# Two distances from the weights, modulo 256 bytes, for the operands of the split fp32r matmuls

## The chip, the cores and the metric

The kernel runs on one core of a Trainium2 chip. The metric is the device time of one execution in microseconds, on the slowest core, which here is the only one. Three timed executions of the kernel before took 1705.59, 1720.77 and 1727.60 us; their median, 1720.77 us, is the time before. A fourth execution was profiled.

## What is computed

Two transformer blocks over one sequence of 256 tokens of width 1024, in float32. What matters for this change are the six feed-forward stages; between them stand three mixers (an mLSTM with a spatial gating unit, a pooling and SSD mixer, and a latent attention) and two final norms.

```python
def swiglu(x, w_in, w_out):
    gate, up = jnp.split(x @ w_in, 2, axis=-1)
    return (jax.nn.silu(gate) * up) @ w_out

x = x + 0.5 * swiglu(rmsnorm(x, ffn1_norm_g[l]), ffn1_w_in[l], ffn1_w_out[l])
```

`D_MODEL` is 1024 and `D_FF` is 2816, so one stage multiplies the 256 tokens by 1024 x 5632 and by 2816 x 1024 weights.

## The kernel before

**Stages.** `PHASES` lists eleven stages, numbered n = 0 to 10: feed-forward stages at n = 0, 2, 4, 6, 7 and 9, the mixers at 1, 5 and 8, the final norms at 3 and 10. Activations lie transposed: channels on the 128 partitions, tokens along the free dimension, so `x` is 128 x 8 x 256.

**Weights.** They come as one stream of blocks of 128 x 2048 float32 (1 MB each). A feed-forward stage has 33 blocks: 11 steps of one gate block, one up block and one out block. Each block is loaded into one of three slots of `raw`. ScalarE then rounds it to fp32r into `whi` (line 176), and VectorE writes the rest, `raw - whi`, into `wlo` (line 184).

**Split matmuls.** To keep float32 precision, each product is made of three fp32r matmuls, `PASSES`: high weights by high activations, high weights by low activations, low weights by high activations. In `pe_in` (line 252, gate and up) the moving operand is `xh`, `xl`, `xh` in turn; in `pe_out` (line 284) it is `hid_hi`, `hid_lo`, `hid_hi`. The stationary operand is a 128 x 128 piece of `whi` or `wlo`. Each matmul has its own weight load and streams 256 columns of 4 bytes. One block is 48 such matmuls, and a stage is 33 x 48 = 1584, the six stages 9504. The first gate block of a stage goes through line 244, in another order of the same three products.

**What sets the order.** It is written out by hand with semaphores, and in a feed-forward stage steps 1 to 10 are five turns of a hardware loop of two steps each (`pe.Fori(1, 5)` after a first turn). In a step TensorE runs gate, up and out blocks one behind the other without a pause if the blocks are split in time.

**Where the tiles lie.** SBUF addresses follow the order of the declarations. In bytes of one partition, `whi` and `wlo` start 24,576 apart (a multiple of 256), `xh` starts 88,512 bytes behind `whi` and `xl` 8,192 further; `hid_hi` starts 132,800 bytes behind `whi` and `hid_lo` 4,096 further. 88,512 and 132,800 are both 192 more than a multiple of 256. The pieces of a weight block start at multiples of 512 bytes and the rows of the activations at multiples of 1,024, so in every matmul of lines 244, 252 and 284 the moving operand lies 192 bytes, modulo 256, behind the stationary one. `hid_hi` and `hid_lo` are tiles of a region that the mixers use again for their own tiles; those lie at the same distance of 192. In `pe_tok` (line 267) the roles are exchanged, the weights stream and `xh`, `xl` are stationary, so there the moving operand is at distance 64.

Of the kernel before, what the change touches and what calls it, by code (L numbers as in the profile page):

```python
# [29 lines left out]
P = 128  # L30
T = 256
D = 1024
KD = D // P
# [23 lines left out]
MOD_GROUPS = {0: 5, 1: 5, 2: 5, 3: 3, 4: 0, 5: 0}  # L57


PARAMS = [("g_ffn1", 8), ("g_mix", 8), ("g_ffn2", 8), ("g_final", 8), ("conv_w1", 64), ("conv_b1", 16),  # L60
          ("b_i", 1), ("b_f", 1), ("head_g", 8), ("sgu_bs", 128), ("mod_b", 144), ("norm_g2", 48),
          ("pool_scale", 4), ("conv_w2", 48), ("conv_b2", 12), ("dt_bias", 1), ("a_log", 1), ("ssd_d", 8),
# [6 lines left out]
def offsets(table):  # L69
    at, o = {}, 0  # L70
    for name, width in table:
        at[name] = (o, o + width)
        o += width
    return at, o


def build_program(nc, a_x, a_pos, a_stream, a_mod, a_params, a_consts, a_sgu, a_out, phases=PHASES):
    F32, F32R, I32 = mybir.dt.float32, mybir.dt.float32r, mybir.dt.int32
    ALU, ACT, AX = mybir.AluOpType, mybir.ActivationFunctionType, mybir.AxisListType
    ds = bass.ds  # L80
    P_AT, P_N = offsets(PARAMS)
    C_AT, C_N = offsets(CONSTS)
    first_block, b0 = [], 0
    for _, _, nb in phases:
        first_block.append(b0)
        b0 += nb
# [3 lines left out]
    with ExitStack() as ctx:  # L90
        def sb(name, shape, dt=F32):
            return ctx.enter_context(nc.sbuf_tensor(name, shape, dt))
# [3 lines left out]
        def sem(name):  # L96
            if name not in sems:
                sems[name] = ctx.enter_context(nc.semaphore(name))
            return sems[name]
# [5 lines left out]
        mod_raw = sb("mod_raw", [P, 2, BLK])  # L105
        mod_acc = sb("mod_acc", [P, D])
        mod_tab = sb("mod_tab", [P, 144])
        mod_part = sb("mod_part", [P, 5, 32])
        fold = sb("fold", [P, 32])
        ident_b = sb("ident_b", [P, P], mybir.dt.bfloat16)  # L110
        mask_b = sb("mask_b", [P, P], mybir.dt.bfloat16)
# [6 lines left out]
        xm = sb("xm", [P, KD, T])  # L118
        gmod = sb("gmod", [P, KD])
        gres = sb("gres", [P, KD])  # L120
        xh = sb("xh", [P, KD, T], F32R)
        xl = sb("xl", [P, KD, T], F32R)
        std = sb("std", [P, T])
        rstd = sb("rstd", [P, T])
        params = sb("params", [P, P_N])
# [8 lines left out]
        def region(**tensors):  # L134
            with ExitStack() as here:
                return [here.enter_context(nc.sbuf_tensor(name, shape, dt)) for name, (shape, dt) in tensors.items()]

        gate, hid, hid_hi, hid_lo, mod_turned = region(gate=([P, 2, T], F32), hid=([P, 2, T], F32),
                                                       hid_hi=([P, 2, 2, T], F32R), hid_lo=([P, 2, 2, T], F32R),
                                                       mod_turned=([P, 32, 32], F32))  # L140


        bank = [ctx.enter_context(nc.psum_tensor(f"bank{i}", [P, 512], F32)) for i in range(8)]
# [10 lines left out]
        def cst(name):  # L154
            lo, hi = C_AT[name]
            return consts[:, lo:hi]
# [202 lines left out]
        def pe_norm(pe, n):  # L359
            if n > 0 and phases[n - 1][0] == "final":  # L360
                pe.wait_ge(sem("x_updated"), 4 * n)
            for b in range(4):
                if b == 0 and n > 0:
                    pe.wait_ge(sem("silu_done"), STEPS * sum(kind == "ffn" for kind, _, _ in phases[:n]))
                if b >= 2:
                    pe_keep_warm(pe, n, WARM[b - 2])
                pe.wait_ge(sem("x_paired"), 4 * n + b + 1)
                for tt in range(2):
                    mm = pe.matmul(STAT[:, T + tt:T + tt + 1], xm[:, 2 * b, tt * P:tt * P + P], ones[:, 0:1],  # L369
                                   start=(b == 0 and tt == 0), stop=(b == 3), skip_group_check=True)  # L370
            mm.then_inc(sem("x_summed"), 1)
            pe_keep_warm(pe, n, WARM[2])
            pe.wait_ge(sem("rstd_ready"), n + 1)
            for tt in range(2):
                mm = pe.matmul(STAT[:, tt * P:tt * P + P], rstd[:, tt:tt + 1].to_broadcast([P, P]), ident,
                               start=(tt == 0), stop=True, skip_group_check=True)
            mm.then_inc(sem("rstd_spread"), 1)
            if phases[n][0] != "final":
                pe_keep_warm(pe, n, WARM[3])
            elif n + 1 < len(phases):  # L380
                pe_keep_warm(pe, n, 60)
# [53 lines left out]
        for n, (kind, idx, _) in enumerate(phases):  # L435
            if kind != "final":
                split_index[n] = k_split
                k_split += 1
                if kind in ("mix2", "mix3"):
                    shift_index[n] = k_shift  # L440
                    k_shift += 1
# [184 lines left out]
        group0, g = {}, 0  # L626
# [1339 lines left out]
        @block.sync  # L1966
        def _(sp):
            for i in range(2):
                sp.dma_start(x[:, 4 * i:4 * i + 4, :], a_x[:, 4 * i:4 * i + 4, :]).then_inc(sem(f"x_loaded{i}"), 16)
            sp.dma_start(consts[:, :], a_consts).then_inc(sem("consts_loaded"), 16)  # L1970
            sp.dma_start(params[:, 0:4 * KD], a_params[:, 0:4 * KD]).then_inc(sem("consts_loaded"), 16)
            for n in range(min(SLOTS, N_BLOCKS)):
                sp.dma_start(raw[:, n, :], a_stream[n * P:n * P + P, :]).then_inc(sem(f"w_loaded{n}"), 16)
            sp.dma_start(params[:, 4 * KD:P_N], a_params[:, 4 * KD:P_N]).then_inc(sem("params_loaded"), 16)
            full = N_BLOCKS // SLOTS

            def load(s, turn):
                sp.wait_ge(sem("w_lo_ready"), s - SLOTS + 1 + SLOTS * turn)
                sp.dma_start(raw[:, s, :], a_stream[ds(s * P + SLOTS * P * turn, P), :])\
                  .then_inc(sem(f"w_loaded{s}"), 16)  # L1980

            if full > 1:
                with sp.Fori(1, full) as turn:
                    for s in range(SLOTS):
                        load(s, turn)
            for s in range(N_BLOCKS % SLOTS):
                load(s, full)
            sp.wait_ge(sem("x_updated"), 4 * (len(phases)))
            sp.dma_start(a_out, x[:, :, :]).then_inc(sem("stored"), 16)
            sp.wait_ge(sem("stored"), 16)  # L1990
# [32 lines left out]
        @block.tensor  # L2023
        def _(pe):
            pe.wait_ge(sem("zeros_ready"), 1)
            for _ in range(60):
                pe.matmul(GATE[:, 0:P], row_parts[:, 0:P], row_parts[:, 0:P], start=True, stop=True)
            pe.wait_ge(sem("consts_loaded"), 32)
            pe.wait_ge(sem("masks_ready"), 3)
            for n, (kind, f, _) in enumerate(phases):  # L2030
                if n == 1:
                    pe.wait_ge(sem("params_loaded"), 16)
                PE[kind](pe, n, f)

        @block.scalar
        def _(act):
            act.wait_ge(sem("eps_ready"), 2)
            for n, (kind, f, _) in enumerate(phases):
                ACTS[kind](act, n, f)

        @block.vector
        def _(dve):
            dve.memset(row_parts[:, :], 0.0).then_inc(sem("zeros_ready"), 1)
            dve.memset(cols[:, 64:65], RMS_EPS).then_inc(sem("eps_ready"), 1)
            dve.memset(cols[:, 65:66], LN_EPS).then_inc(sem("eps_ready"), 1)
            dve.wait_ge(sem("consts_loaded"), 32)
            dve.tensor_copy(ident_b[:, :], ident).then_inc(sem("masks_ready"), 1)
            dve.tensor_copy(mask_b[:, :], cst("maskT")).then_inc(sem("masks_ready"), 1)
            dve.tensor_copy(row_of3[:, :], cst("row_of3")[0:96, :]).then_inc(sem("masks_ready"), 1)
            dve.tensor_reduce(fold[:, :], ident.rearrange("p (q i) -> p i q", q=4), AX.X, ALU.add)\  # L2050
               .then_inc(sem("fold_ready"), 1)
            for n, (kind, f, _) in enumerate(phases):
                DVE[kind](dve, n, f)


# [59 lines left out]
def _params(v):  # L2115
# [11 lines left out]
    def conv(w):  # L2127
# [16 lines left out]
          "sgu_wT": v["sgu_w_s"][0].transpose(2, 0, 1).reshape(P, -1)}  # L2144
    return np.concatenate([at[name].reshape(P, width) for name, width in PARAMS], axis=1)

# [44 lines left out]
```

## Time and profile before

| | before |
|---|---|
| median of 3 executions | 1720.77 us (1705.59 to 1727.60) |
| profiled execution | 1711.11 us |
| its span, first to last instruction | 1709.4 us |
| TensorE matmul busy | 1675.8 us (98%) |
| VectorE / ScalarE / GpSimd busy | 1201.2 / 809.4 / 85.1 us |
| mean granted TensorE clock | 0.991 |
| DMA | 365.08 MB, mean 214 GB/s |

The page gives busy time of each engine, the span in 40 slices, the chain of work that ended last, and the costliest groups of instructions by line. A matmul's recorded duration includes its way through the array and overlaps the next one's, so the distance from one start to the next says more about throughput than the duration does. In the chain of work, neighbouring pieces of one line are merged, and their time divided by their count is that distance.

### The profile page before, as it was taken

The numbers are of one execution on the slowest core, as the hardware profiler recorded it, in microseconds if no ns is written. First come the engines' busy times: TensorE is split into PE (matmuls) and PEld (weight loads), VectorE is DVE, ScalarE is ACT, GpSimd is POOL, SyncE is SP. The second block draws the span as 40 slices with busy tenths as digits, with TensorE's granted clock in tenths as the row PEclk, the third lists the DMA queues.
The fourth block names the chain that finished last, engine by engine and source line by source line (L and its number), as shares of the span: only waits on it lengthen the run. The fifth ranks groups of instructions, "written<-read, shape, count | busy, mean of one in ns | idle before, by whom it ended". The sixth has DMA issues, their size and how long they took to land.

```text
span 1709.4 us, 34392 instructions
## 1 busy us (share of the span) xinstructions
PE 1675.8 (98%) x14512; PEld 1641.4 (96%) x14512; DVE 1201.2 (70%) x1303; ACT 809.4 (47%) x874; POOL 85.1 (5%) x110
## 2 busy tenths in 40 slices
PE   9999999999999999999998999999999999999998
PEld 9999999999999999999997899999999988899998
DVE  5888875676788877878866778646555666764544
ACT  5444556644544344343565543435434455554342
POOL 0000000000000000000012000000000003100000
PEclk8999999999999999999999999999999999999999
DMA  7998754444498856888442368643555433345551
GB/s 311 344 340 308 265 176 171 147 150 164 176 347 325 326 214 230 318 323 304 177 149 102 122 249 320 242 175 138 208 203 189 170 123 128 126 168 191 179 196 50
DMA packets 50491, 365.08 MB, mean 214 GB/s; under 512 B 5728, under 2 KB 5856, under 8 KB 6240
## 3 DMA queue, kind: packets, MB, share of 16 engines
q1 hardware_dynamic: 39744, 287.04, 46.0%
q0 software_dynamic: 10368, 75.50, 11.9%
q8 instruction: 74, 1.21, 0.3%
q10 hardware_dynamic: 288, 1.18, 0.2%
q14 instruction: 17, 0.14, 0.0%
HBM read 362.65 MB, written 1.05 MB: 213 GB/s over the span
## 4 chain that ended last, share of the span: by engine, by line
PE 88%; DVE 7%; ACT 3%; issue 1%; DMA 0%; SPq 0%; ACTq 0%; DVEq 0%
PE bank L252 50%; PE bank L284 24%; PE bank L267 3%; PE bank L244 2%; DVE wlo L184 2%; PE bank L357 2%; PE bank L369 1%; PE bank L1661 1%; ACT whi L176 1%; DVE m_e L1923 1%; DVE m_p L1426 1%; ACT m_e L1802 0%; DVE xm L401 0%; DVE x L309 0%; PE bank L1619 0%
## 5 line engine op out<-in xcount | busy, mean ns | idle before, releaser
L184 DVE TENSOR_TENSOR wlo<-raw,whi 128x2048 fp32r<-128x2048 f32 x261 | 598.2, 2294 | 209.3 <-ACT whi L176 208.9
L252 PE MATMUL bank<-xh,whi 128*128 128x256 f32 x2608 | 729.6, 280 | 2.7 <-DVE wlo L184 1.4
L252 PE MATMUL bank<-xl,whi 128*128 128x256 f32 x2608 | 726.4, 279 | 0.0
L252 PE MATMUL bank<-xh,wlo 128*128 128x256 f32 x2608 | 726.3, 278 | 0.0
L176 ACT ACTIVATE whi<-raw 128x2048 fp32r<-128x2048 f32 x261 | 497.9, 1912 | 313.2 <-PE bank L252 187.4
L252 PEld LDWEIGHTS bank<-xh,whi 128*128 128x128 f32 x2608 | 492.2, 189 | 5.4 <-issue 2.8
L252 PEld LDWEIGHTS bank<-xh,wlo 128*128 128x128 f32 x2608 | 493.1, 189 | 0.0
L252 PEld LDWEIGHTS bank<-xl,whi 128*128 128x128 f32 x2608 | 490.4, 188 | 0.1
L284 PE MATMUL bank<-hid_hi,whi 128*128 128x256 f32 x1056 | 294.5, 279 | 0.0
L284 PE MATMUL bank<-hid_lo,whi 128*128 128x256 f32 x1056 | 294.1, 278 | 0.0
L284 PE MATMUL bank<-hid_hi,wlo 128*128 128x256 f32 x1056 | 294.1, 278 | 0.0
L284 PEld LDWEIGHTS bank<-hid_hi,wlo 128*128 128x128 f32 x1056 | 199.7, 189 | 0.0
L284 PEld LDWEIGHTS bank<-hid_hi,whi 128*128 128x128 f32 x1056 | 198.9, 188 | 0.4
L284 PEld LDWEIGHTS bank<-hid_lo,whi 128*128 128x128 f32 x1056 | 198.2, 188 | 0.0
L534 ACT ACTIVATE hid_hi<-hid 128x512 fp32r<-128x512 f32 x66 | 41.8, 633 | 283.1 <-DVE hid L563 283.1
L578 DVE SCALAR_TENSOR_TENSOR mod_acc<-mod_raw,c_act,mod_acc 128x1024 f32<-128x1024 f32 x126 | 161.6, 1282 | 2.6
L563 DVE TENSOR_TENSOR hid<-gate,bank 128x512 f32<-128x512 f32 x66 | 45.3, 686 | 81.9 <-PE bank L252 81.7
L1996 POOL DMA_DIRECT2D mod_raw<-mod_in x72 | 38.3, 532 | 937.0 <-DVE mod_acc L578 925.3
L565 DVE TENSOR_TENSOR hid_lo<-hid,hid_hi 128x512 fp32r<-128x512 f32 x66 | 45.7, 693 | 46.2 <-ACT hid_hi L534 46.2
L357 PE MATMUL bank<-ident_b 128*128 128x128 bf16 x690 | 49.5, 229 | 0.0
L357 PEld LDWEIGHTS bank<-ident_b 128*128 128x128 bf16 x690 | 46.7, 108 | 0.2
L659 DVE SCALAR_TENSOR_TENSOR m_pre<-bank,params,m_pre 128x255 f32<-128x255 f32 (+2 forms) x84 | 34.0, 474 | 14.9 <-ACT m_pre L646 14.9
(315 smaller groups left out, 1812.2 us busy)
## 6 DMA issues: line engine op xcount, KB each, us to landing
raw<-stream_in SPq DMA_DIRECT2D x270, 1024.0 KB, 4.8
mod_raw<-mod_in POOLq DMA_DIRECT2D x72, 1024.0 KB, 6.6
params<-params_in SPq DMA_DIRECT2D x1, 1474.0 KB, 16.0
x<-x_in SPq DMA_DIRECT2D x2, 512.0 KB, 4.4
m_gsu<-sgu_in ACTq DMA_DIRECT2D x1, 1024.0 KB, 5.1
y_out<-x SPq DMA_DIRECT2D x1, 1024.0 KB, 3.8
consts<-consts_in SPq DMA_DIRECT2D x1, 280.5 KB, 4.8
tab_pos<-pos_in ACTq DMA_DIRECT2D x1, 128.0 KB, 2.6
```

The source lines that it names most:

```text
L176: act.activation(whi[:, s, :], raw[:, s, :], ACT.Copy).then_inc(sem("w_hi_ready"), 1)
L184: dve.tensor_tensor(wlo[:, s, :], raw[:, s, :], whi[:, s, :].bitcast(F32), ALU.subtract)\
L244: last = pe.matmul(out[:, m, :], w[:, s, c:c + P], (xh, xl)[part][:, k, :], start=(part == 0 and k == 0 and m == 0 and w is whi), stop=(pa ...
L252: last = pe.matmul(out[:, m, :], (whi, wlo)[wp][:, s, k * 256 + m * P:k * 256 + m * P + P], (xh, xl)[ap][:, k, :], start=(k == 0 and j == ...
L267: last = pe.matmul(out[:, tt, :], (xh, xl)[ap][:, k, tt * P:tt * P + P], (whi, wlo)[wp][:, s, k * 256:k * 256 + 256], start=(k == 0 and j ...
L284: mm = pe.matmul(pair(acc[d // 2])[:, d % 2, :], (whi, wlo)[wp][:, s, c:c + P], (hi, lo)[ap][:, kt, :], start=(first and d % 2 == 0 and kt ...
L357: pe.matmul(bank_[:, 0:P], ident_b[:, :], ident_b[:, :], start=True, stop=True, skip_group_check=True)
L534: act.activation(hid_hi[:, parity], hid[:, :, :], ACT.Copy).then_inc(sem("hid_rounded"), 1)
L563: dve.tensor_tensor(hid[:, :, :], gate[:, :, :], pair(UP), ALU.mult).then_inc(sem("hid_ready"), 1)
L565: dve.tensor_tensor(hid_lo[:, parity], hid[:, :, :], hid_hi[:, parity].bitcast(F32), ALU.subtract)\
L578: ins = dve.scalar_tensor_tensor(out=mod_acc[:, :], in0=mod_raw[:, s, t * D:t * D + D], scalar=c_act[:, k:k + 1], in1=mod_acc[:, :], op0=A ...
L1996: pool.dma_start(mod_raw[:, s, :], a_mod[ds(s * P + 2 * P * turn, P), :])\
```

## The change

`xh`, `xl`, `hid_hi` and `hid_lo` are declared 64 elements (256 bytes) larger, and before each stage a function `place(n)` sets the views through which that stage sees them, on TensorE, ScalarE and VectorE alike. The view starts 0, 16, 32 or 48 elements (0, 64, 128 or 192 bytes) into the room, by the table `STARTS`. `mod_part` moves from the fixed part of SBUF into the region, and a tile `room_before_region` that nothing uses is added. No instruction is added, removed or moved, and no shape changes; only addresses do.

```diff
+ROOM = 64
+STARTS = {0: (32, 0, 32, 0), 1: (32, 32, 0, 0), 2: (32, 48, 16, 0), 3: (32, 32, 0, 0), 4: (32, 16, 48, 0), 5: (32, 32, 0, 0),
+          6: (0, 48, 16, 32), 7: (0, 16, 48, 32), 8: (32, 32, 0, 0), 9: (48, 16, 48, 16), 10: (32, 32, 0, 0)}
...
-        mod_part = sb("mod_part", [P, 5, 32])
...
-        xh = sb("xh", [P, KD, T], F32R)
-        xl = sb("xl", [P, KD, T], F32R)
+        xh_room = sb("xh", [P, KD * T + ROOM], F32R)
+        xl_room = sb("xl", [P, KD * T + ROOM], F32R)
+        sb("room_before_region", [P, 32])
...
-        gate, hid, hid_hi, hid_lo, mod_turned = region(gate=([P, 2, T], F32), hid=([P, 2, T], F32),
-                                                       hid_hi=([P, 2, 2, T], F32R), hid_lo=([P, 2, 2, T], F32R),
-                                                       mod_turned=([P, 32, 32], F32))
+        gate, hid, hi_room, lo_room, mod_turned, mod_part = region(
+            gate=([P, 2, T], F32), hid=([P, 2, T], F32), hid_hi=([P, 4 * T + ROOM], F32R), hid_lo=([P, 4 * T + ROOM], F32R),
+            mod_turned=([P, 32, 32], F32), mod_part=([P, 5, 32], F32))
+
+        def moved(room, k, start):
+
+            return room[:, start:start + k * T].rearrange("p (k t) -> p k t", k=k)
+
+        xh, xl, hid_hi, hid_lo = None, None, None, None
+
+        def place(n):
+
+            nonlocal xh, xl, hid_hi, hid_lo
+            h, l, g, r = STARTS[n]
+            xh, xl = moved(xh_room, KD, h), moved(xl_room, KD, l)
+            hid_hi = moved(hi_room, 4, g).rearrange("p (q m) t -> p q m t", q=2)
+            hid_lo = moved(lo_room, 4, r).rearrange("p (q m) t -> p q m t", q=2)
```

With the declared sizes, the distances behind the weights modulo 256 bytes become these:

| stage n | xh | xl | hid_hi | hid_lo |
|---|---|---|---|---|
| all stages before | 192 | 192 | 192 | 192 |
| 0 | 192 | 64 | 64 | 192 |
| 2 | 192 | 0 | 0 | 192 |
| 4 | 192 | 128 | 128 | 192 |
| 6 | 64 | 0 | 0 | 64 |
| 7 | 64 | 128 | 128 | 64 |
| 9 | 0 | 128 | 128 | 0 |
| 1, 3, 5, 8, 10 | 192 | 192 | 192 | 192 |

So each feed-forward stage gets one of the six pairs of different distances, and the mixers and final norms keep the distance they had. The constants and the region with the mixers' tiles keep their addresses; `x`, `xm` and the small tiles ahead of them move by 640 bytes.

## Rows read from the trace of the kernel before

**Rows 1.** The page: busy time by engine, and TensorE's share and granted clock by slice.
```profile
PE 1675.8 (98%) x14512; PEld 1641.4 (96%) x14512; DVE 1201.2 (70%) x1303; ACT 809.4 (47%) x874; POOL 85.1 (5%) x110
PE   9999999999999999999998999999999999999998
PEclk8999999999999999999999999999999999999999
```
**Rows 2.** The page: the chain that ended last, share of the span by engine and line.
```profile
PE 88%; DVE 7%; ACT 3%; issue 1%; DMA 0%; SPq 0%; ACTq 0%; DVEq 0%
PE bank L252 50%; PE bank L284 24%; PE bank L267 3%; PE bank L244 2%; DVE wlo L184 2%; PE bank L357 2%; PE bank L369 1%; PE bank L1661 1%; ACT whi L176 1%; DVE m_e L1923 1%; DVE m_p L1426 1%; ACT m_e L1802 0%; DVE xm L401 0%; DVE x L309 0%;
```
**Rows 3.** The chain in order of time (start us, us, what), stages 0 to 9.
```profile
177.73 10.88 PE bank L252 x96
188.61 8.16 PE bank L284 x72
...
602.96 10.88 PE bank L252 x96
...
804.92 11.31 PE bank L252 x96
816.23 8.48 PE bank L284 x72
...
1147.39 11.31 PE bank L252 x96
...
1334.95 10.88 PE bank L252 x96
...
1675.19 11.31 PE bank L252 x96
```
**Rows 4.** Groups by line between 47 and 190 us (busy us, mean ns).
```profile
L252 PE MATMUL bank<-xl,whi 128*128 128x256 f32 x288 | 79.5, 276 | 0.0
```
**Rows 5.** Groups by line between 669 and 824 us.
```profile
L252 PE MATMUL bank<-xl,whi 128*128 128x256 f32 x288 | 80.9, 281 | 0.0
```
**Rows 6.** The chain in order of time, start of stage 4.
```profile
646.51 5.45 PE bank L252 x48
...
655.25 2.30 DVE wlo L184
657.56 0.14 issue
657.69 5.89 PE bank L252 x48
663.59 5.65 PE bank L284 x48
```
**Rows 7.** The chain in order of time, inside the first mixer, where line 267 exchanges roles.
```profile
220.17 34.13 PE bank L252 x288
254.30 16.96 PE bank L267 x144
...
293.37 5.45 PE bank L267 x48
```
**Rows 8.** Timeline of TensorE ahead of stage 2 (start us, us, what).
```profile
441.96 1.61 PE L357 MATMUL bank<-ident_b 128*128 128x128 bf16 x26
```
**Rows 9.** Timeline of TensorE in the third mixer, 24 matmuls of 512 columns.
```profile
1403.24 0.40 PE L1637 MATMUL bank<-whi,xh 128*128 128x512 f32 x1
...
1408.53 0.39 PE L1637 MATMUL bank<-wlo,xh 128*128 128x512 f32 x1
```

More of the change, by code:

```diff
@@ L2032, in _ @@
                     pe.wait_ge(sem("params_loaded"), 16)
+                place(n)
                 PE[kind](pe, n, f)
@@ L2038, in _ @@
             for n, (kind, f, _) in enumerate(phases):
+                place(n)
                 ACTS[kind](act, n, f)
@@ L2052, in _ @@
             for n, (kind, f, _) in enumerate(phases):
+                place(n)
                 DVE[kind](dve, n, f)
```

## The prediction

> **What bounds the kernel now.** I read the engines' busy time first: TensorE's matmuls are busy for 98% of the span at a granted clock of nearly full speed from the second slice on, while VectorE stands at 70% and ScalarE at 47% [rows 1]. Then the chain of work that ended last: 88% of it is TensorE, and lines 252 and 284, the split matmuls, make 50% and 24% of the span [rows 2]. So the time of this kernel is the number of these matmuls times the distance from one start to the next. Nothing here is gained by a wait removed; only that distance counts.
>
> Then the same chain in order of time, where time over count gives the distance. In stage 0, 96 matmuls of line 252 take 10.88 us, 113.3 ns each, and 72 of line 284 take 8.16 us, again 113.3 ns. In stage 4 the same code takes 11.31 us and 8.48 us, 117.8 ns each. Stages 2 and 7 read like stage 0, and stages 6 and 9 like stage 4 [rows 3]. The reader is to see that there are two states and nothing between them, 4.5 ns apart, though all addresses, shapes and code are the same in all six stages. It shows in the matmuls' own durations too, 276 against 281 ns [rows 4, 5], so the matmul itself is stretched, and does not wait for another engine. A state holds for a whole loop of some 150 us, whatever the other engines and the DMAs do meanwhile.
>
> Where does a state begin? In stage 4, a block runs at 5.45 us for 48 (113.5 ns). TensorE then waits for a split of line 184, and the next blocks take 5.89 us (with the restart in it) and 5.65 us (117.8 ns) [rows 6]. So the state is taken at the restart after a pause and is kept while the stream is unbroken. One stage is 1584 matmuls, or 16.5 times the 96 of rows 3, and the states differ by 0.43 us per 96: one stage in the other state is 7.1 us. The profiled execution has three stages in each. The four executions known are 1705.6, 1711.1, 1720.8 and 1727.6 us, in steps of 5.5, 9.7 and 6.8 us. That is what a varying number of such stages and mixer pieces would give; it is my reading, and the timed executions have no trace.
>
> **The change, part by part.** The sums start from the profiled execution, 1711.1 us, which is the span of 1709.4 and 1.7 us around it. It lies 9.7 us below the median of the three timed executions.
>
> *No instruction changes.* The loads, splits, waits and matmuls of before stand in the same order; `place(n)` only sets addresses when the program is built. Cost nothing, and no cover is needed.
>
> *`mod_part` moved, the empty tile, `x` and `xm` shifted by 640 bytes.* VectorE and ScalarE read and write these. Were VectorE's pieces slower by a few per cent, the idle time of an engine at 70% would take it [rows 1]. What is not covered is the chain's 7% on VectorE and 3% on ScalarE, at the norms [rows 2]: some 170 us in all, so 1% of slowing there would be 1.7 us. I take nothing, because no access pattern changes but its start. The mixers keep their distances.
>
> *The distance of the moving operand in the 9504 matmuls.* This is the whole change. What the trace shows of other distances is little. In line 267 the weights stream and the activations are stationary, so the moving operand lies at 64 and not at 192. There, 144 matmuls take 16.96 us (117.8 ns), joined without a pause to 288 of line 252 at 118.5 ns; later, after a pause, 48 take 5.45 us (113.5 ns) [rows 7]. So a second distance has the same two states with the same two values, and the switch from one distance to the other in an unbroken stream (rows 7, at 254.30 us) did not leave the state. That is the nearest evidence, and it says that the distance as such changes nothing. Distances 0 and 128, and the alternation of two distances within three matmuls, no row shows. I bound them:
>
> - From below: the 26 bf16 matmuls of 128 columns take 1.61 us from the first start to the last end; less one duration of 0.22 us, 25 distances are 1.39 us, 55.7 ns each [rows 8]. Another 128 columns at the granted full clock (2.4 GHz) are 53.3 ns, so 256 columns without any hindrance would be some 109 ns, an estimate. Against the mean of the six stages, (113.3 + 117.8) / 2 = 115.55 ns, that is 6.55 ns by 9504, a gain of 62 us.
> - From above: in line 1637, 24 fp32r matmuls of 512 columns start within 5.29 us, 230.0 ns apart [rows 9], and by the same estimate 512 unhindered columns would be 55.7 + 3 x 53.3 = 215.6 ns. The excess is 14.4 ns. Were that the excess of each matmul of 256 columns, they would stand at 123.4 ns: 7.85 ns by 9504, a loss of 75 us.
>
> Between ends so far apart I take the value of the nearest row, that of rows 7: the same two states. So the sum is 1711.1 + 0, with a new draw of states: all six stages at 113.3 ns would be 1711.1 - 3 x 7.1 = 1690 us, all six at 117.8 ns 1732 us. The middle of the four executions known, of which each is such a draw, is (1711.1 + 1720.8) / 2 = 1716 us.
>
> The Trainium skill, "TensorE: Matmul & The Clock Gate", section "Step-by-step: what each phase is for", says that the moving operand and the weight load have independent read ports, so that loading the next weights does not take bandwidth from the running matmul. By that rule addresses could not matter at all, and the sum would be the same 1716 us. The trace agrees only in part, since the fp32r matmuls are stretched in a way that the rule has no room for (276 or 281 ns, rows 4 and 5). The same page, section "Wait — 56ns, not 53.3ns?", gives N over 2.4 GHz plus about 2.5 ns for back-to-back matmuls; for 256 columns that is 109.2 ns, by which 62 us would lie idle in this kernel. The bf16 matmuls agree with it (55.7 ns), the fp32r ones do not (113.3 and 117.8 ns).
>
> **The rivals.**
>
> *A. The stream is freed.* If the stretch comes from the matmul's and the weight load's reads meeting at one place of a 256-byte pattern, a second distance could separate them in part of the passes. For it: fp32r matmuls stand 4 to 9 ns above 109, and something makes two states. Against it: distance 64 has the same states as 192. Price: fully freed, 1711 - 62 = 1649 us; halfway between 113.3 and 109 (111.2 ns), 4.35 x 9504 = 41 us, 1670 us. It decides for faster by 2% (below 1686.4) once the mean is under 113.0 ns, better than the better state of today.
>
> *B. Alternating distances break the lock.* A state that repeats exactly for 150 us looks like a rhythm in which each matmul meets its weight load at the same offset. With two distances, each switch between high and low activations changes the offset, and the reads could collide anew. The place is lines 252 and 284, two switches in every three matmuls. Price up to the bound above, 1711 + 75 = 1786 us. It decides for slower by 2% (above 1755.2) from a mean of 120.2 ns on. For it: one pass out of step already costs 4.5 ns in the worse of the two rhythms. Against it: the switch of distance in rows 7.
>
> *C. The better state always.* A second distance could make only the rhythm of 113.3 ns stable: 1690 us, within 2%.
>
> *D. The worse state always.* The mirror image: 1732 us, within 2%.
>
> *E. Nothing depends on the distance*, and the change does not do what it says. This is the forecast itself in its purest form, and gives 1716 us with the spread of before.
>
> **How the numbers follow.** The forecast with E, the two states drawn anew, gets 0.40; C gets 0.10, D 0.12, A 0.22, B 0.16. The six pairs are all different, so A and B may both hold in different stages and cancel in part, which also speaks for a small sum. The predicted time is that of the forecast, 1716 us; its own range is 1695 to 1735. A measurement of this kernel can tell about 2% from no change, that is 1686.4 to 1755.2. Faster is A, 0.22; slower is B, 0.16; the same is the rest, 0.62. The range goes from 1668, at the half-way price of A, to 1755, the near edge of B, and leaves out about half of A and most of B.
>
> **What would show it.** In the chain in order of time, the 96 matmuls of line 252 in each of the stages 0, 2, 4, 6, 7, 9: 10.88 or 11.31 us each for the forecast; under 10.8 for A; over 11.5 for B; 10.88 in all for C, 11.31 in all for D. A time between the two that holds for a whole stage would show that the pair of distances sets the rhythm and that my draw of states is wrong. The durations should stay 276 or 281 ns. The mixers' lines should read as before. The prediction falls if any distance gives a third value, since it rests on one other distance alone.

## The result, and the profile after

| | before | after |
|---|---|---|
| median, executions run side by side | 1712.81 us (9, the three told of at the start among them, from 1697.00 to 1727.60) | 1731.27 us (9, from 1727.66 to 1740.26) |
| ratio, with its 95% interval | | 1.0127 (1.0091 to 1.0162) |
| profiled execution, span | 1709.4 us | 1731.7 us |
| TensorE matmul busy | 1675.8 us | 1700.3 us |

The change makes the kernel slower by 1.3%. That is within 2%, inside the stated range, and clear of the noise; the forecast had been no change. A single execution could not have told this, since 1731 us also lies in the forecast's own range of 1695 to 1735 us; but all nine executions of after are slower than the slowest of before. The spread of the executions has also shrunk, from 31 us to 13 us.

The page of after, as [rows 1] and [rows 2] of before. TensorE is busy for the same 98% of the span and its part of the chain is 91%, up from 88%; it is the time of its matmuls that has grown.

```profile
PE 1700.3 (98%) x14512; PEld 1666.0 (96%) x14512; DVE 1202.0 (69%) x1303; ACT 808.8 (47%) x874; POOL 85.1 (5%) x110
PE 91%; DVE 5%; ACT 2%; issue 1%; DMA 0%; SPq 0%; DVEq 0%; ACTq 0%
```

The chain of after in order of time (start us, us, what), which answers to [rows 3]. Lines 271 and 303 are 252 and 284 of before. The stages 0, 2, 4, 6, 7 and 9 follow each other.

```profile
182.83 11.31 PE bank L271 x96
194.14 8.43 PE bank L303 x72
...
614.64 11.45 PE bank L271 x96
...
818.54 11.40 PE bank L271 x96
829.94 8.71 PE bank L303 x72
...
1164.25 11.40 PE bank L271 x96
...
1357.21 11.30 PE bank L271 x96
...
1697.18 11.31 PE bank L271 x96
1708.49 11.48 PE bank L303 x96
```

No stage reads 10.88 us any more. 11.40 and 11.45 us (118.8 and 119.3 ns each) and 8.71 us (121.0 ns) are values that before did not have. Stages 0, 2 and 7 stood at 113.3 ns before and lose most: over 11 times 96 matmuls of line 271, 0.43 us each in stage 0 is 4.7 us, 0.57 us in stage 2 is 6.3 us, 0.42 us in stage 7 is 4.6 us. The three stages that already stood at 117.8 ns lose 1 us or less there, and line 303 adds the rest. The spans differ by 22.3 us. Taken from the first to the last of their 1584 matmuls, the six stages are together 24.7 us longer, and all the rest of the span is 2.4 us shorter.

### The profile page after: what moved, and what is told of

It is laid out like the page before. It is cut to its first block, busy times and chain, and to the rows that moved or that the text cites. A ratio compares the mean times of both kernels' runs of the same rounds, so it can differ in the third digit from the quotient of the medians.

```text
span 1731.7 us, 34392 instructions
## 1 busy us (share of the span) xinstructions
PE 1700.3 (98%) x14512; PEld 1666.0 (96%) x14512; DVE 1202.0 (69%) x1303; ACT 808.8 (47%) x874; POOL 85.1 (5%) x110
## 4 chain that ended last, share of the span: by engine, by line
PE 91%; DVE 5%; ACT 2%; issue 1%; DMA 0%; SPq 0%; DVEq 0%; ACTq 0%
PE bank L271 52%; PE bank L303 24%; PE bank L263 3%; PE bank L286 3%; PE bank L376 2%; PE bank L1680 1%; DVE wlo L203 1%; PE bank L388 1%; DVE m_p L1445 0%; DVE x L328 0%; PE bank L1691 0%; DVE x L420 0%; PE bank L1249 0%; PE bank L1638 0%; ACT m_e L1821 0%
```

## The experiments

Each ratio below is to the kernel before, run side by side with the version in question. Three theories were carried at first. **1**: equal distances keep a rhythm, and two different ones break it, whatever their values. **2**: the value of the distance sets the rhythm. **3**: the loss comes from what else moved.

### Everything moved, all distances at 192

```diff
-STARTS = {0: (32, 0, 32, 0), 1: (32, 32, 0, 0), 2: (32, 48, 16, 0), ...
+STARTS = {n: (32, 32, 0, 0) for n in range(11)}
```

> The changed kernel with its rooms, the moved mod_part and the empty tile, but all four tiles at distance 192 in all stages. Theory 1 and 2: as before, each stage at 113.3 or 117.8 ns and a time of 1697 to 1728 us. Rival 3 (the loss comes from what else has moved, such as x, xm and mod_part): 1727 to 1740 us, as the change.

Measured: ratio to before 1.0004 (0.9971 to 1.0038), ten executions from 1703.8 to 1723.8 us. The moved tiles cost nothing, and theory 3 falls. In its trace two stages (0 and 9) stand at 113.3 ns and four at 117.8 ns, not the same ones as in before. So the two values belong to no stage; with the same distances they fell on other stages in this execution.

### Two distances for xh and xl alone

```diff
-STARTS = {0: (32, 0, 32, 0), ..., 2: (32, 48, 16, 0), ...
+STARTS = {0: (32, 0, 0, 0), ..., 2: (32, 48, 0, 0), ...
```

> The change for xh and xl alone; hid_hi and hid_lo stay at 192 in all stages. Lines 263 and 271 should have the values of the change (117.7 to 119.3 ns). Theory 1 with a rhythm that equal distances find again by themselves: line 303 at 113.3 or 117.8 ns, settled within a few matmuls of each out block, and some 1720 to 1732 us. Theory 1 with a rhythm that is found only after a pause: line 303 keeps odd values between 116 and 121 ns.

Measured: ratio 1.0066 (1.0036 to 1.0096), median 1723.3 us. The chain in order of time, stages 0, 4 and 6:

```profile
181.80 11.30 PE bank L270 x96
193.10 8.16 PE bank L302 x72
...
812.05 11.41 PE bank L270 x96
823.46 8.16 PE bank L302 x72
...
1155.53 11.40 PE bank L270 x96
1166.94 8.48 PE bank L302 x72
```

Gate and up blocks (line 270) read as in the change. As the first form of the expectation had it, the out blocks (line 302), all at 192, fall to 113.3 ns in five of the six stages, at once and without a pause between; only in stage 6 (distances 64 and 0 ahead of them) do they come out at 117.8 ns. So the stream does not have to stop to find a rhythm. What runs ahead of it seems to decide which one it finds; one trace with one stage that differs does not show that.

The time of this version is between before and the change, yet the loss does not divide in the same way. Its gate and up blocks have the whole loss of the change there: 118.4 ns on average over the six stages, against 115.6 ns before, which by 6336 matmuls is some 18 us. Its out blocks are quicker than before, 114.2 ns on average against 115.6 ns, and give some 4 us back. In the change line 303 gives nothing back but adds some 9 us of its own.

### One distance per stage, of four values

```diff
-STARTS = {0: (32, 0, 32, 0), ..., 2: (32, 48, 16, 0), ...
+STARTS = {0: (48, 48, 16, 16), ..., 2: (0, 0, 32, 32), ..., 4: (16, 16, 48, 48), ..., 6: (32, 32, 0, 0),
+          7: (48, 48, 16, 16), ..., 9: (0, 0, 32, 32), ...
```

> The changed kernel with one distance per stage for all four tiles, but not the same in each stage: 0 in stages 0 and 7, 64 in stages 2 and 9, 128 in stage 4, 192 in stage 6. Theory 1 (two different distances break a rhythm that needs equal ones; the value does not matter): every stage has all its split matmuls at 113.3 or at 117.8 ns, nothing else, and the time is that of before, 1697 to 1728 us. Theory 2 (the values 0, 64 and 128 are themselves bad, 192 is good): only stage 6 reads 113.3 or 117.8 ns, the others have values of their own between 117 and 121 ns, and the time stays near 1730 us.

Measured: ratio 1.015 (1.0111 to 1.019), median 1738.8 us: as slow as the change within the noise, with no two distances in one stage. In the two traces the six stages take 1128.9 and 1128.7 us together. The chain in order of time, stages 0, 2, 4, 6, 7 and 9, with distances 0, 64, 128, 192, 0 and 64:

```profile
185.52 11.52 PE bank L270 x96
...
620.43 11.31 PE bank L270 x96
...
826.47 11.39 PE bank L270 x96
...
1164.02 10.88 PE bank L270 x96
...
1359.55 11.52 PE bank L270 x96
...
1699.75 11.31 PE bank L270 x96
```

Distance 0 gives 120.0 ns both times, 128 gives 118.6 ns, 64 gives 117.8 ns both times, and in this trace only 192 gives 113.3 ns. Theory 1 falls and theory 2 holds. What this run leaves open is whether 64 always gives 117.8 ns: in [rows 7] it read 113.5 ns too.

### Separate streams

TensorE alone, 72 matmuls after each pause, all else left out; the tile named in the row sets the distance.

```python
for k in range(72):
    c, t = (k // 3) % 16 * P, (k // 3) % 8 * 256
    mm = pe.matmul(bank[n % 2][:, 0:N], whi[:, c:c + P], moving[...][:, t:t + N], start=(k == 0), stop=(k == 71), ...)
```

> Not the computation: 57 separate streams of 72 fp32r matmuls with a pause and 8 small bf16 matmuls ahead of each; nothing else runs meanwhile, and the output is the input. The first 33 streams have one moving tile each, at distances 0, 32, ... 224 bytes from the weights modulo 256 (tiles on, by_a to by_g), four draws of each. Then 12 streams that take their moving operand in turn from two tiles (a, b, a), at all ordered pairs of 0, 64, 128 and 192; then streams of 512 and of 128 columns, and streams with one unchanging stationary piece. Theory 1: the first 33 at 113.3 or 117.8 ns whatever the distance, both values at most distances; the pairs at 116.7 to 121.1 ns, as in the stages of the change. Theory 2: the value goes with the distance and repeats in its four draws. If the weight load's reads are what stretches the matmul, streams of 128 columns stand further above 128 columns of clock (53.3 ns) in proportion than those of 512 (213.3 ns).

The timeline of TensorE. Each row is one stream of 72: 71 distances from start to start and one duration of about 0.28 us. First one draw (one stream after its own pause) of each distance 0, 32, 64, 96, 128, 160, 192 and 224, then a later draw of 64 and 192, then streams of 512 and of 128 columns at 192 and at 0:

```profile
117.94 8.87 PE L117 MATMUL bank<-on,whi 128*128 128x256 f32 x72
127.68 8.65 PE L117 MATMUL bank<-by_a,whi 128*128 128x256 f32 x72
137.23 8.41 PE L117 MATMUL bank<-by_b,whi 128*128 128x256 f32 x72
146.58 8.88 PE L117 MATMUL bank<-by_c,whi 128*128 128x256 f32 x72
156.42 8.79 PE L117 MATMUL bank<-by_d,whi 128*128 128x256 f32 x72
165.99 8.70 PE L117 MATMUL bank<-by_e,whi 128*128 128x256 f32 x72
175.50 8.42 PE L117 MATMUL bank<-by_f,whi 128*128 128x256 f32 x72
184.76 8.76 PE L117 MATMUL bank<-by_g,whi 128*128 128x256 f32 x72
...
213.83 8.72 PE L117 MATMUL bank<-by_b,whi 128*128 128x256 f32 x72
...
252.31 8.73 PE L117 MATMUL bank<-by_f,whi 128*128 128x256 f32 x72
...
464.43 17.04 PE L117 MATMUL bank<-by_f,whi 128*128 128x512 f32 x72
482.36 16.59 PE L117 MATMUL bank<-on,whi 128*128 128x512 f32 x72
499.89 8.23 PE L117 MATMUL bank<-by_f,whi 128*128 128x128 f32 x72
509.09 8.23 PE L117 MATMUL bank<-on,whi 128*128 128x128 f32 x72
```

Settled, over the last 24 matmuls of a stream, the four draws of each distance give:

| distance | 0 | 32 | 64 | 96 | 128 | 160 | 192 | 224 |
|---|---|---|---|---|---|---|---|---|
| ns | 120.0 | 116.7 or 117.8 | 113.3 or 117.8 | 120.0 | 118.8 | 117.4 or 118.8 | 113.3 or 117.8 | 118.3 |

So of these eight distances only 64 and 192 ever reach 113.3 ns, and the prediction's one other distance was the other good one. That again is theory 2. Streams that keep one stationary piece throughout read the same as those that change it every three matmuls, 120.0 ns at distance 0 and 117.8 ns at 192 (two draws each). The streams that alternate two distances, over the same stretch, stand below beside the stages of the change (mean start to start within the blocks, from the second to the ninth out block of the stage), first for line 271, then for line 303:

| moving operand in turn (line 271) | 192, 64, 192 | 192, 0, 192 | 192, 128, 192 | 64, 0, 64 | 64, 128, 64 | 0, 128, 0 |
|---|---|---|---|---|---|---|
| separate stream, ns | 117.8 | 119.3 | 118.9 | 118.9 | 117.8 | 117.8 |
| stage of the change, ns | 117.8 | 119.3 | 118.7 | 118.8 | 117.7 | 117.8 |

| moving operand in turn (line 303) | 64, 192, 64 | 0, 192, 0 | 128, 192, 128 | 0, 64, 0 | 128, 64, 128 | 128, 0, 128 |
|---|---|---|---|---|---|---|
| separate stream, ns | 117.8 | 117.8 | 121.1 | 120.0 | 118.9 | 120.0 |
| stage of the change, ns | 117.1 | 117.9 | 121.1 | 117.7 | 116.8 | 119.1 |

The six pairs of line 271 agree within 0.2 ns. Nothing but TensorE runs in the separate streams, so no other engine and no DMA takes part in what they show. In them only the moving operand's address differs from stream to stream; the weights always start at a multiple of 256 bytes. By the streams alone it could be the moving address that counts and not the distance. Line 267 speaks against that: there the weights are the moving operand, at the same multiple of 256 as distance 0 in the streams, and the stationary operand is the one that lies at 192. If the moving address alone counted, it would read 120.0 ns. It reads 117.8 and 113.5 ns in [rows 7], and in the trace of the change, as line 286, 144 matmuls take 16.32 us (113.3 ns). That is what distance 64 gives in the streams, so both addresses count. The out blocks agree in three cases within 0.7 ns and are 0.9 to 2.3 ns quicker in the others; they are only 48 matmuls long and are entered from another pair, and how much of the gap that explains was not tried. None of the twelve ordered pairs reached 113.3 ns. Of the streams of other widths, those of 128 columns take 111.7 ns at either distance, far above the 53.3 ns of 128 columns at 2.4 GHz, while those of 512 columns are 6 to 9% above their 213.3 ns. That is what was expected if the weight load holds them up.

### Between the multiples of 32

Distances are set by taking the view a few elements further into a tile.

> Not the computation: 56 streams of 72 fp32r matmuls after a pause, at distances between the multiples of 32 bytes, two draws each: 48, 56, 68, 72, 80, 88, 176, 184, 196, 200, 208, 216, 16, 112, 144, 240; then 0, 256, 192 and 448; then at 0 and 192 with stationary pieces of 96 and 64 columns, and with 384 and 192 moving columns. Theory 2 (distance modulo 256 sets the rhythm): 256 reads as 0 (120.0 ns) and 448 as 192 (113.3 or 117.8 ns); a few distances near 64 and 192 may give 113.3 ns in every draw. If the pattern is finer than 256 or coarser, 256 and 448 differ from 0 and 192. Theory 6 (the weight load of 128 columns, 111.7 ns, is the floor): with 64 or 96 stationary columns the 256-column matmuls fall below 113.3 ns, towards 109.

The timeline of TensorE: distances 112, 0, 256, 192 and 448 with 128 stationary columns, then 0 with 64.

```profile
160.07 8.45 PE L117 MATMUL bank<-room_d,whi 128*128 128x256 f32 x72
...
343.57 8.87 PE L117 MATMUL bank<-room_a,whi 128*128 128x256 f32 x72
353.37 8.87 PE L117 MATMUL bank<-room_a,whi 128*128 128x256 f32 x72
363.20 8.43 PE L117 MATMUL bank<-room_g,whi 128*128 128x256 f32 x72
372.41 8.42 PE L117 MATMUL bank<-room_g,whi 128*128 128x256 f32 x72
...
429.67 8.36 PE L117 MATMUL bank<-room_a,whi 128*64 128x256 f32 x72
```

256 reads as 0 (120.0 ns) and 448 as 192 (113.3 or 117.8 ns): in these two cases the pattern repeats after 256 bytes. Of the sixteen distances in between only 112 reached 113.3 ns, in both draws; the others lay between 116.7 and 122.2 ns. With 64 stationary columns, distance 0 fell from 120.0 to 113.3 ns, but 192 rose to 119.0 ns, so a shorter weight load moves the rhythm and does not simply free it. Moving operands of 192 columns take 111.7 ns at distances 0 and 192, the same as 128 columns, and those of 384 columns take 173.3 ns at both. Nothing with 256 moving columns went below 113.3 ns; the expected fall towards 109 ns did not come.

### Can the good rhythm be forced?

> Not the computation: 45 streams, each four pieces of 24 fp32r matmuls of 256 columns at distance 192 (tile by_f) with nothing between the pieces but a steering insertion: none, one to three matmuls at distance 0, one or two at 128, one at 64, one or two of 128 columns, one of 64 or of 512 columns, weights of 32 or 64 columns, one or three small bf16 matmuls; three draws of each, after a pause. Theory 4 (the rhythm is set by where the two read streams stand to each other, and is kept until something shifts them): without insertion all four pieces of a stream are alike, 113.3 or 117.8 ns; with one, some kinds lead to 113.3 ns in every piece whatever the piece before was. Rival 5 (the rhythm is drawn by chance at each shift): each kind gives both values in some order, and no kind gives one alone in nine pieces.

The timeline of TensorE: pieces of 24 at distance 192 (by_f), with one matmul at distance 128 (by_d) between. The first piece after a pause takes 3.07 us when it settles at 117.8 ns and some 2.99 us when it settles at 113.3 ns; a piece behind this insertion that settles at 113.3 ns takes 2.89 to 2.91 us.

```profile
176.51 3.07 PE L117 MATMUL bank<-by_f,whi 128*128 128x256 f32 x24
179.42 0.29 PE L125 MATMUL bank<-by_d,whi 128*128 128x256 f32 x1
179.54 2.91 PE L117 MATMUL bank<-by_f,whi 128*128 128x256 f32 x24
182.29 0.28 PE L125 MATMUL bank<-by_d,whi 128*128 128x256 f32 x1
182.41 2.89 PE L117 MATMUL bank<-by_f,whi 128*128 128x256 f32 x24
```

Without insertion, a stream kept its value through all 96 matmuls in three of three. One or three matmuls at distance 0, one or two at 128, two of 128 columns, and weights of 32 or 64 columns were each followed by 113.3 ns in nine of nine pieces; three small bf16 matmuls by 117.8 ns in nine of nine. Others led to both values, some by strict turns: two at distance 0, or one of 512 columns, changed the rhythm at each of nine insertions, so it is not chance that rules at each shift (rival 5). So it looked as if the rhythm could be set. The evidence was thinner than "nine of nine" sounds, since most of these pieces followed one that was at 113.3 ns already. Over the seven kinds ten insertions met 117.8 ns, and all ten ended it; for the one matmul at distance 128 it was a single one, the first in the rows above. In the kernel the rhythm could not be set. The matmul was put into the kernel before, in two places per stage:

```diff
+        def pe_steer(pe, s):
+            pe.matmul(STAT[:, 0:T], whi[:, s, 0:P], xh[:, :, :].rearrange("p k t -> p (k t)")[:, 48:48 + T],
+                      start=True, stop=True, skip_group_check=True)
```

> The kernel before with two more matmuls in each feed-forward stage, after the third pair of passes of the up block of step 1 and of the gate block of step 2: 256 columns of xh taken 192 bytes further (distance 128 instead of 192), into a PSUM bank that nothing reads then. Theory 4 (one matmul at distance 128 puts the stream in the rhythm of 113.3 ns, which then holds): all six stages at 113.3 ns in the trace, no 117.8 ns in their loops, and 1690 to 1700 us in every execution, whatever the draw; against the median of before some 15 to 20 us less. Rival 5 (chance at each shift): the two values as before, 1703 to 1730 us.

> The same places, with three bf16 matmuls of 128 columns in place of the one at distance 128. In the separate streams these left 117.8 ns behind them in all nine pieces. Theory 4: all six stages at 117.8 ns, 1728 to 1740 us in every execution. Rival 7 (any insertion after the last pause helps, because it lets the stream settle): as steered, 1690 to 1700 us.

Measured: steered 0.9958 (0.9929 to 0.9987), twelve executions from 1695.0 to 1718.7 us; in its trace four stages stay at 117.8 ns. With the bf16 matmuls 0.991 (0.9875 to 0.9946), four executions from 1692.2 to 1711.6 us, with two stages at 117.8 ns, where theory 4 had all six. Both expectations missed. The starts of the matmuls in the rhythm of 117.8 ns (118, 117, 118 ns apart and so on, in whole ns) allow a pattern that repeats after three. Every first insertion of the streams stood behind 24 matmuls, a multiple of three, and might have met the same one of three beats each time. That was tried next, as theory 4 with beats.

> Not the computation: 15 streams at distance 192 of five pieces each, with one matmul at distance 128 between the pieces, the pieces 24 matmuls long in five streams, 25 in five, 26 in five; then eight draws each of plain streams of 72 at distances 112 and 192, then three draws each at 100, 104, 108, 116, 120 and 124. Theory 4 with beats (the rhythm of 117.8 ns repeats after three matmuls, and the insertion ends it only if it falls on the right one of three): in the streams of 24, whose insertions fall 25 apart, and of 25, whose fall 26 apart, a piece at 117.8 ns ends at 113.3 ns after one to three insertions; in the streams of 26, whose insertions fall 27 apart, a stream that starts at 117.8 ns either ends it at the first insertion or never. Pieces at 113.3 ns stay there. Distance 112: 113.3 ns in all eight draws, if its advantage is that it has one rhythm only; 192: both values among eight.

> As steered, but with three matmuls at distance 128 in the gate block of step 2 alone, four matmuls apart, so that they fall on all three beats of the rhythm of 117.8 ns. Theory 4 with beats: all six stages at 113.3 ns from there on, 1688 to 1700 us in every execution. If the insertion does not end the rhythm here at all, some stages stay at 117.8 ns as in steered, and the time at 1695 to 1719 us.

In the streams of five pieces at 192, all pieces at 113.3 ns stayed there. Of the four streams that began at 117.8 ns, two changed at the first insertion and one at the second, but one, with insertions 25 apart, stayed at 117.8 ns through all four. In the kernel, with insertions on three beats, one stage left 117.8 ns there (stage 0) and four did not; ratio 0.9967 (0.9932 to 1.0003), ten executions from 1696.5 to 1719.1 us. So both expectations missed again, and three beats are not the whole of it. Which condition lets an insertion work was not found, and the small gains of steered and steered_off have no shown cause.

### One distance of 112

The same run of short streams also had single streams of 72 at 112 (near), at 192 (room) and at distances around 112 (near again). In its timeline, the first draw of 112, the first of 192 and the first of 116:

```profile
261.25 8.46 PE L118 MATMUL bank<-near,whi 128*128 128x256 f32 x72
270.60 8.73 PE L118 MATMUL bank<-room,whi 128*128 128x256 f32 x72
443.36 9.01 PE L118 MATMUL bank<-near,whi 128*128 128x256 f32 x72
```

Distance 112 settled at 113.3 ns in eight of eight draws, 192 in three of eight, and 100, 104, 108, 116, 120 and 124 never. The kernel with 112 in the six feed-forward stages:

```diff
+STARTS = {0: (12, 12, 44, 44), 1: (32, 32, 0, 0), 2: (12, 12, 44, 44), ..., 4: (12, 12, 44, 44), ...
```

> The changed kernel with all four tiles at one distance of 112 bytes in the feed-forward stages, 192 elsewhere; no instruction added. The two separate streams at 112 settled at 113.3 ns, after some fifteen matmuls. Theory 2 with a distance that has one rhythm: all six stages at 113.3 ns, 1690 to 1703 us in every execution. If 112 has two rhythms like 64 and 192 and two draws were luck: stages at a second value too, and 1700 us or more.

Measured: ratio 0.9876 (0.9845 to 0.9907), median 1690.8 us, four executions from 1686.6 to 1693.1 us, at and just under the low end of what was expected. The chain in order of time, stages 0, 2, 4, 6, 7 and 9:

```profile
175.59 10.88 PE bank L270 x96
186.47 8.16 PE bank L302 x72
...
599.88 10.88 PE bank L270 x96
...
794.94 10.88 PE bank L270 x96
...
1131.87 10.88 PE bank L270 x96
...
1318.76 10.88 PE bank L270 x96
...
1651.44 10.88 PE bank L270 x96
```

All six stages stand at 113.3 ns. So 112 is worth having because in all its draws here it had one rhythm and not two. This version beats both kernels: 1.2% under before, clear of the noise, and, by the two ratios, 2.5% under the change.

> As at_112, with xh and xl at 112 in the second and third mixer too (stages 5 and 8; the first mixer streams the weights and stays at 192). Theory 2: the blocks of line 271 there, 48 matmuls after a pause each, settle at 113.3 ns but take some fifteen matmuls to do so, which costs about what half of them at 117.8 ns cost before: the time is that of at_112, 1687 to 1693 us, within 2 us.

Measured: ratio 0.989 (0.985 to 0.993), median 1691.0 us over six executions, as expected no different from at_112. The six stages of its trace stand at 113.3 ns too.

## Why the prediction was wrong

**What bounds the kernel** held. The distance from start to start of the split matmuls is the time, and there are two rhythms at distance 192, taken anew after pauses and kept in the loop. The run with everything moved shows them in other stages than before. What did not hold is that there are only these two: 118.8 and 119.3 ns, each held for a whole stage, are third values, and by its own words the prediction falls if any distance gives one.

**"No instruction changes" and the moved tiles at nothing** held, at 1.0004 (0.9971 to 1.0038).

**The step that failed** is "Between ends so far apart I take the value of the nearest row, that of rows 7: the same two states". Rows 7 show distance 64, and from them the text concluded "that the distance as such changes nothing". The streams show that 64 is the one other multiple of 32 that reaches 113.3 ns; 0, 32, 96, 128, 160 and 224 never do. One row at another distance could not tell a flat line from two equal points on a curve. The bounds of the unknown were worked out, and then a value at zero was put in for their inside. In its place the runs showed some 2.7 ns a matmul: 118.3 ns on average in the stages of the change against 115.6 ns before. Rival E, that nothing depends on the distance, falls with it.

**The size.** By 9504 matmuls, the step from 115.6 to some 118.3 ns is 26 us against the profiled execution before. The stages are 24.7 us longer from first to last matmul. The spans differ by 22.3 us, since the rest took 2.4 us less, most of it in the first mixer, which drew better rhythms this time (288 matmuls of line 271 in 32.86 us and 144 of line 286 in 16.32 us, against 34.13 and 16.96 us in [rows 7]).

**The rivals.** D named 1732 us, and 1731.27 us was measured, but its mechanism, 117.8 ns in all stages, holds only for some of the pairs. B named the place and the direction, but not the mechanism: it blamed the two switches in every three matmuls, and the run with one distance per stage, without any such switch, is as slow. C was priced at 1690 us, and the kernel at 112 shows that price: 1690.8 us. It was looked for in a second distance and lay in another single one. A's 1649 us cannot be reached by addresses alone as far as these runs go: its 109 ns came from bf16 matmuls, and fp32r matmuls with 128 stationary columns take 111.7 ns even with 128 moving columns.

By the rule of the Trainium skill on independent read ports ("TensorE: Matmul & The Clock Gate", section "Step-by-step: what each phase is for") loading the next weights takes no read bandwidth from the running matmul. For fp32r the separate streams speak against it, and the measurement decides: with TensorE alone at work, the moving operand's place against the weights moves the distance from start to start between 113.3 and 122.2 ns, and at distance 0 a weight load of 64 columns in place of 128 takes it from 120.0 to 113.3 ns. Where the two reads meet no run here shows.

## What to carry to other kernels

When a kernel is a chain of back-to-back matmuls, divide time by count stage by stage before anything else: two values for the same code were a lead worth some 20 us here. Test such a lead on the operand pair alone, in short streams over many distances, before any is built into the kernel; one point beside the present one says nothing on the curve. Prefer an address with one rhythm to one with two, even where the better rhythm is the same.

## What the runs showed of the hardware

- An fp32r matmul of 256 columns with its own load of 128 weight columns, at a granted clock of 0.998 to 1.000, stands 113.3 to 122.2 ns from the next, by the distance of its moving operand from the weights modulo 256 bytes, in steps as fine as 4 bytes: 108 gives 120.0 ns, 112 gives 113.3 ns, 116 gives 121.8 ns.
- At distances 64 and 192 the same stream has two rhythms, 113.3 and 117.8 ns, and keeps the one that it has while nothing comes between. Some other distances have two as well (32: 116.7 and 117.8 ns; 160: 117.4 and 118.8 ns), while 112 gave 113.3 ns in ten of ten streams and in all twelve stages of two traces.
- With 512 columns the order turns round: 226.7 ns at distance 0, 233.3 ns at 192, settled.
- fp32r matmuls of 128 columns with 128 stationary columns take 111.7 ns at either distance, twice the 55.7 ns of the bf16 ones [rows 8]. Those of 192 columns take 111.7 ns as well, so up to there the moving columns are not the limit. The weight load is the likely one; short streams with fewer stationary columns were not run.
